# Expert stage of a streaming-encoder trunk: activation turned on VectorE, down products in quarters, combine one item later, gather for four items at once

## The reference

```python
def moe_swiglu(h, w_router, w_gate, w_up, w_down):
    logits = xt @ w_router
    top_logit, top_idx = lax.top_k(logits, TOP_K)          # TOP_K = 2 of 8
    gates = jax.nn.softmax(top_logit, axis=-1)
    ...
    def expert_block(args):
        tok, e = args
        xb = xt[tok]                                       # gather the frames
        return (jax.nn.silu(xb @ w_gate[e]) * (xb @ w_up[e])) @ w_down[e]
    ...
    contrib = y_rows[pos] * gates[:, None]                 # combine
    y = jax.ops.segment_sum(contrib, flat_tok, num_segments=n_tok)
```

## Time and profile before

| | us |
|---|---|
| median of 3 runs | 1605.27 |
| their ends | 1601.61 to 1605.38 |
| the profiled execution | 1601.6 |
| its span, first to last instruction | 1599.8 |

### The profile page before, as it was taken

The page is one execution under the profiler, slowest core; times in us unless marked ns, Lnnn a source line. Parts: engine busy times, 40 slices in busy tenths (PEclk is TensorE's granted clock), DMA queues, the critical chain, the costliest instruction groups (busy, mean ns, idle before and its releaser), DMA issues.

```text
span 1599.8 us, 30459 instructions
## 1 busy us (share of the span) xinstructions
PE 1528.5 (96%) x13157; PEld 844.9 (53%) x13157; DVE 399.6 (25%) x610; ACT 377.0 (24%) x524; POOL 24.0 (1%) x42
## 2 busy tenths in 40 slices
PE   4999899999899869999999999999999999999996
PEld 3977899999799753333333333333333333333332
DVE  3454554444466651001001001001001001001001
ACT  4333544444467521001001001001001001011001
POOL 1000000000011100000000000000000000000000
PEclk9999999999999989999999999999999999999998
DMA  9430555555353357997997998997998998998960
GB/s 301 161 128 19 180 184 185 184 185 184 109 168 106 106 227 291 372 413 298 371 416 296 380 400 300 381 406 299 380 398 306 376 403 298 386 396 300 394 244 28
DMA packets 132553, 438.31 MB, mean 274 GB/s; under 512 B 10602, under 2 KB 63936, under 8 KB 116032
## 3 DMA queue, kind: packets, MB, share of 16 engines
q1 hardware_dynamic: 131232, 432.73, 72.3%
q0 software_dynamic: 1184, 3.50, 0.7%
HBM read 435.15 MB, written 1.05 MB: 273 GB/s over the span
## 4 chain that ended last, share of the span: by engine, by line
PE 93%; DVE 2%; ACT 2%; issue 1%; DMA 1%; SPq 1%; DVEq 0%; POOL 0%; ACTq 0%
PE bank L1121 55%; PE bank L764 9%; PE bank L765 9%; PE bank L766 9%; PE bank L1191 3%; PE bank L1175 2%; PE bank L1154 2%; DMA raw<-in_ev_w_in 1%; PE bank L864 1%; PE bank L757 1%; ACT high L594 1%; DVE hn L1523 0%; SPq L707 0%; DVE low L599 0%; PE bank L1165 0%
## 5 line engine op out<-in xcount | busy, mean ns | idle before, releaser
L1121 PE MATMUL bank<-ring,arena 128*32 128x512 f32 (+1 forms) x8832 | 878.9, 556 | 0.8 <-ACT arena L1404 0.8
L1121 PEld LDWEIGHTS bank<-ring,arena 128*32 128x32 f32 x8832 | 280.4, 110 | 561.3 <-issue 561.3
L599 DVE TENSOR_TENSOR low<-raw,high 128x2048 fp32r<-128x2048 f32 x74 | 169.3, 2290 | 169.5 <-ACT high L594 169.5
L764 PE MATMUL bank<-ht_h,high 128*128 128x256 f32 x672 | 192.5, 287 | 3.0 <-DVE vec L1587 3.0
L765 PE MATMUL bank<-ht_l,high 128*128 128x256 f32 x672 | 191.1, 284 | 0.0
L766 PE MATMUL bank<-ht_h,low 128*128 128x256 f32 x672 | 191.0, 284 | 0.0
L594 ACT ACTIVATE high<-raw 128x2048 fp32r<-128x2048 f32 x74 | 141.5, 1912 | 162.9 <-PE bank L766 158.1
L1898 DVE TENSOR_TENSOR arena<-arena,bank 128x512 f32<-128x512 f32 (+1 forms) x48 | 29.8, 621 | 536.6 <-PE bank L1121 535.1
L764 PEld LDWEIGHTS bank<-ht_h,high 128*128 128x128 f32 x672 | 129.9, 193 | 4.4 <-issue 3.9
L765 PEld LDWEIGHTS bank<-ht_l,high 128*128 128x128 f32 x672 | 130.1, 194 | 0.2
L766 PEld LDWEIGHTS bank<-ht_h,low 128*128 128x128 f32 x672 | 129.9, 193 | 0.0
(11 more groups left out here) (264 smaller groups left out, 1075.1 us busy)
## 6 DMA issues: line engine op xcount, KB each, us to landing
ring<-in_moe_w_down SPq DMA_DIRECT2D x112, 1024.0 KB, 8.0
ring<-in_moe_w_gate SPq DMA_DIRECT2D x64, 1024.0 KB, 7.3
ring<-in_moe_w_up SPq DMA_DIRECT2D x64, 1024.0 KB, 7.0
ring<-in_moe_w_gate SPq DMA_DIRECT2D x64, 768.0 KB, 5.6
ring<-in_moe_w_up SPq DMA_DIRECT2D x64, 768.0 KB, 7.3
raw<-in_ffn_w_gate SPq DMA_DIRECT2D x14, 1024.0 KB, 5.0
raw<-in_ffn_w_up SPq DMA_DIRECT2D x14, 1024.0 KB, 5.0
raw<-in_ffn_w_down SPq DMA_DIRECT2D x14, 1024.0 KB, 4.9
```

The lines of the kernel that those rows point to most:

```text
L599: nc.vector.tensor_tensor(low[:, n % SPLITS, :], raw[:, raw_slot(n), :], high[:, n % SPLITS, :].bitcast(F32), ALU.subtract).then_inc(split ...
L764: mm(out, l_high, r_high, start=start, stop=False)
L1121: ins = mm(ps(use)[q * GRP:(q + 1) * GRP, 0:width], lhs(r, q), rhs(q), start=first, stop=last_piece)
```

## The change

- **Turning.** VectorE transposes the activation in 32x32 blocks straight into `m_act_t` after multiplying it. For that the gate and up products read their weights in runs of 32 columns, quarter by quarter, so that a block holds 32 columns of one quarter. TensorE's `act_transposes` and ScalarE's `turned_acts` go.
- **Down.** Each quarter q now makes 256 output columns over all contraction blocks: 3 groups x 2 blocks x 4 quarters = 24 products of 256 columns for a piece, 48 matmul instructions. One chain of sums over both parts; ScalarE copies three 128x256 results to `y_e`, and `y_first` goes.
- **Combine.** 24 products, 256 wide, with 32 rows of contraction, in the next item behind its second gate piece; the last one stands behind both loops.
- **Gather.** For items 0 to 3 ahead of item 0, for items 4 to 7 inside it, with one-pass products of `hn` split in a high and a low part (384 columns, four for each of eight blocks). VectorE copies an item's rows from `xg_all` to `xg`. The split is a ScalarE copy and a POOL subtraction of 128x2048.
- **Loop.** Item 0 is written out ahead of the loop, `Fori(1, NE)`. Extra items gather on their own (`gather_extra`).

```diff
+DN = DM // NQ
+DOWN_ORDER = (2, 0, 1)
+DOWN_BANKS = {0: 6, 1: 7, 2: 2}
+FIRST_ITEMS = NE // 2
+GATHERED = FIRST_ITEMS * SLOTS
...
@@ TensorE
             def expert_gate_up(j, item):
...
+                weights = ring[:, at:at + NQ * width].rearrange("p (b q i) -> p q b i", q=NQ, i=GRP)
                 pe.wait_ge(*expert_landed(j, item))
-                tiled(product(key), part, key, lambda r, q: xg[:, k, r * GRP:(r + 1) * GRP],
-                      lambda q: ring[:, at + q * width:at + (q + 1) * width], k == 0, width, item)
+                for r in range(NG):
...
+                        ins = mm(ps(use)[q * GRP:(q + 1) * GRP, 0:width], xg[:, k, r * GRP:(r + 1) * GRP],
+                                 weights[:, q, :, :], start=k == 0, stop=k == DK - 1)
...
             def expert_down(j, item):
...
+                for r in DOWN_ORDER:
+                    use = ("md", r)
+                    if j == 4 * DK:
+                        open_bank(pe, use, item)
+                    for c in range(2):
+                        for q in range(NQ):
+                            ins = mm(ps(use)[q * GRP:(q + 1) * GRP, 0:DN], m_act_t[:, r, first + c, :],
+                                     ring[:, at + c * DM + q * DN:at + c * DM + (q + 1) * DN],
+                                     start=j == 4 * DK and c == 0, stop=ends and c == 1)
...
+            def gather(half, k):
+
+                use = ("gather", half, k)
+                open_bank(pe, use)
+                for t in range(T):
+                    for part in (hn_h, hn_l):
+                        last = mm(ps(use)[:, 0:GATHERED], part[:, t, k * P:(k + 1) * P],
+                                  sel_all[:, t, half * GATHERED:(half + 1) * GATHERED],
+                                  start=t == 0 and part is hn_h, stop=t == T - 1 and part is hn_l)
+                last.then_inc(fill_sem(use), 1)
...
+            def combine(item):
+
+                for r in DOWN_ORDER:
+                    pe.wait_ge(*drained(("md", r), item))
                 for half in range(2):
+                    pe.wait_ge(*drained(("sgt", half), item))
                 for t in range(T):
                     for r in range(NG):
+                        for q in range(NQ):
+                            use = ("mc", q)
+                            if t == 0 and r == 0:
                                 open_bank(pe, use, item)
+                            rows = slice(q * GRP, (q + 1) * GRP)
+                            last = mm(ps(use)[:, t * DN:(t + 1) * DN], sgt[rows, r, t * P:(t + 1) * P], y_e[rows, r, :],
+                                      start=r == 0, stop=r == NG - 1)
+                            if t == T - 1 and r == NG - 1:
                                 last.then_inc(fill_sem(use), 1)
...
+                    if first and j < DK:
+                        gather(1, j)
+                    if key == ("g", 0, 1) and not first:
+                        combine(item - 1)
+                    if key == ("u", 0, 0):
+                        pe.wait_ge(sel_ready, item + 1)
+                        turned_selection(0, item)
+                    if key == ("u", 0, 3):
+                        turned_selection(1, item)
...
+            pe.wait_ge(hn_split, 1)
+            pe.wait_ge(all_sel_ready, T)
+            for k in range(DK):
+                gather(0, k)
+            pe.wait_ge(all_sel_ready, 2 * T)
+            pe.wait_ge(xg_ready, 1)
+            expert_item(0, True)
+            with pe.Fori(1, NE) as item:
+                pe.wait_ge(xg_ready, item + 1)
                 expert_item(item)
             pe.wait_ge(route_ready, 1)
             n_items = pe.value_load(route_i[0:1, 0:1], min_val=NE, max_val=NITEM)
             with pe.Fori(NE, NITEM) as item:
                 with pe.If(n_items > item):
+                    gather_extra(item)
                     expert_item(item)
+            combine(n_items - 1)
@@ ScalarE
             norm_banks(3)
+            act.wait_ge(*filled("router_rows"))
+            act.wait_ge(hn_ready, T * 4)
+            fn(hn_h, hn[:, :, :], ACT.Copy).then_inc(hn_high, 1)
             act.wait_ge(r_in, 1)
             fn(r_e, r_e, ACT.Exp).then_inc(r_exp, 1)
@@ POOL
+            pool.wait_ge(hn_high, 1)
+            nc.gpsimd.tensor_tensor(hn_l, hn[:, :, :], hn_h.bitcast(F32), ALU.subtract).then_inc(hn_split, 1)
+            nc.gpsimd.memset(xg_all[:, NE, :], 0.0).then_inc(past_xg_zero, 1)
@@ VectorE
             def gated(part, item):
...
+                for r in range(NG):
+                    dve.wait_ge(*drained(("mu", part, r), item))
+                    V.transpose(m_act_t[:, r, first:first + blocks, :].rearrange("p b c -> p (b c)"),
+                                m_act[:, r, 0:width]).then_inc(turned_ready, 1)
...
+            def next_rows(item, first=False):
...
+                V.tensor_copy(xg.rearrange("p k s -> p (k s)"), xg_all[:, bass.ds(item + 1, 1), :].rearrange(
+                    "p o c -> p (o c)")).then_inc(xg_ready, 1)
...
+            add_contributions(n_items - 1)
             V.memset(r_max, 0.0).then_inc(experts_done, 1)
```

More of the change, by code:

```diff
@@ L211, in ends_a_product @@
     kind, part, k = key
-    return k == (DPAIRS[part] if kind == "d" else DK) - 1
+    if kind == "d":
+        return (part, k) == (len(PARTS) - 1, DPAIRS[part] - 1)
+    return k == DK - 1
 def ring_places():
@@ L317, in plan_banks @@
     banks.fill("rank", 5)
-    for half in range(2):
-        banks.fill(("gather0", half), 6 + half)
+    for k in range(DK):
+        banks.fill(("gather", 0, k), k)
+    for k in range(DK):
+        banks.fill(("gather", 1, k), 6 + k % 2)
     before = list(banks.count), list(banks.signals)
     for half in range(2):
-        banks.fill(("sgt", half), 6 + half)
+        banks.fill(("sgt", half), 7)
     for part in range(len(PARTS)):
@@ L573, in product @@
             kind, part, _ = key
-            return ("m" + kind, part)
+            return ("md", DOWN_ORDER[-1]) if kind == "d" else ("m" + kind, part, NG - 1)
         def expert_landed(j, item):
@@ L1151, in act_transposes, with turned_selection @@
+            def turned_selection(half, item):
+                use = ("sgt", half)
                 open_bank(pe, use, item)
-                pe.wait_ge(*drained(("mu", part, r), item))
-                for j in range(WIDTHS[part] // P):
-                    last = nc.tensor.transpose(ps(use)[:, j * P:(j + 1) * P], m_act[:, r, j * P:(j + 1) * P], ident)
+                for r in ((0, 1), (2,))[half]:
+                    for t in range(T):
+                        at = (r % 2 * T + t) * P
+                        last = nc.tensor.transpose(ps(use)[:, at:at + P], sel_q[:, t, r * P:(r + 1) * P], ident)
@@ L1168, in gather @@
-            def gather(name, item):
-                for half in range(2):
-                    use = (name, half)
-                    open_bank(pe, use, item)
-                    for k in range(4):
-                        for t in range(T):
-                            last = mm(ps(use)[:, k * SLOTS:(k + 1) * SLOTS],
-                                      hn[:, t, (half * 4 + k) * P:(half * 4 + k + 1) * P], sel[:, t, :],
-                                      start=t == 0, stop=t == T - 1)
-                    last.then_inc(fill_sem(use), 1)
@@ L1194, in combine, with expert_item @@
+                            if t == T - 1 and r == NG - 1:
                                 last.then_inc(fill_sem(use), 1)
-            def expert_item(item):
-                for half in range(2):
-                    b, n, _ = uses[("gather", half)]
-                    pe.wait_ge(s_drained[b], n - bank_fills_per_item[b] + item * bank_fills_per_item[b])
+            def expert_item(item, first=False):
                 for j, key in enumerate(EXPERT_ORDER):
                     kind, part, k = key
-                    if key == ("g", 0, 1):
-                        turned_selection(item)
-                    for p, before in ((0, "g"), (1, "d")):
-                        if (kind, part) == (before, 1 - p) and TURN_AT <= k < TURN_AT + NG:
-                            act_transposes(p, k - TURN_AT, item)
@@ L1892, in gated @@
             def gated(part, item):
+                width, first = WIDTHS[part], PARTS[part][0] // P
+                blocks = width // GRP
                 for r in range(NG):
@@ L1905, in expert_item @@
+            def expert_item(item, first=False):
+                if not first:
+                    add_contributions(item - 1)
+                    for half in range(2):
+                        dve.wait_ge(*filled(("sgt", half), item - 1))
+                one_hot(item)
                 gated(0, item)
                 gated(1, item)
-                for r in range(NG):
-                    use = ("md", 1, r)
-                    dve.wait_ge(*drained(("md", 0, r), item))
-                    dve.wait_ge(*filled(use, item))
```

(18 more changed lines are left out.)

216 lines of the change are left out of this document (115 added, 101 removed).

## The result

| | kernel before | changed kernel |
|---|---|---|
| median of 5 runs, us | 1605.27 (1601.61 to 1606.08) | 1612.87 (1610.79 to 1617.59) |
| ratio to before | 1 | 1.0062, interval 1.0048 to 1.0077 |
| profiled execution: time / span, us | 1601.6 / 1599.8 | 1617.59 / 1615.7 |
| mean granted clock | 0.983 | 0.959 |

What follows compares the result with a forecast made beforehand. TensorE, busy 96% of the span, was taken as the bound. Terms -79.4 + 17.4 + 8.5 + 8.0 + 1.7 + 8.5 = -35.3 us gave 1570 us against the median 1605.27, within 1556 to 1584 (0.53).

Steps and rivals of the forecast that it cites:

- The work of a trip: One trip of TensorE's expert loop: the changed parts together take -9.92 us, a trip of 112.5, -79.4 over eight.
- Gathers in item 0: Gathers of items 4 to 7 inside item 0: eight visits of 1.0 us each, +8.0 us.
- The back branch: End of a loop trip on TensorE: branch no longer hidden, gap of 2.9 us, six branches, +17.4 us (ends 0 and 20).
- The half clock: After back-branch gaps: clock at half for 3.4 us costs 1.7, five of six counted, +8.5 us (ends 0 and 20).
- The cover: Work queued behind TensorE's back branch: twenty instructions of 256 columns, five groups, hiding 1.08 us of it.
- Start of the stage: Before item 0: hn split on ScalarE and POOL, then first gathers; item 0 starts +1.7 us later (ends 0 and 4).
- End of the stage: Last combine behind TensorE's walk over the extra items: 7.3 us on the path, 0.5 for waits; sum +8.5 (+5 to +11).
- The branch stays hidden: Rival at the loop's back branch: no gap and no clock drop, 1544 us; chance 0.14.
- DMA as the bound: Rival in the loop: weight transfers take 119.0 us a trip, seven trips add 15, 1585 us; chance 0.10.
- Two at a time: Rival in the combine: its products run no more than two at a time, +20, 1590 us; chance 0.08.
- slow dispatch: Rival in the down pieces: instructions dispatched too slowly for the quarters, 3.87 us a piece, adding 143, 1713 us; chance 0.06.
- slow operand pattern: Rival in gate and up: runs of 32 elements slow the moving operand, 10% gives 1628 us; chance 0.05.

## Why the prediction was wrong

It named the right mechanism, a back branch that loses its cover, and priced it at a third of what it cost (25.9 of 73.2 us). Point by point:

- **The work of a trip: right.** -9.92 gave 112.48 us, measured 112.59. Down pieces 36.26/14 = 2.59 us (forecast 2.593), combine 2.80 (2.79), no transposes but the selection's (0.59 and 0.37), gate and up unchanged at 5.15 for the first two pieces (2 x 2.576). The line from 512 through 384 columns down to 256 held.
- **Gathers in item 0: right.** Item 0 takes 729.13 - 610.99 = 118.1 us; a clean trip without its combine is 112.59 - 2.80 = 109.8; so 8.3 us, forecast 8.0.
- **The back branch: the step that failed.** Forecast 2.9 us of gap and 1.4 of half clock, 4.3 a trip and 25.9 in all. Measured 5.0 + 3.0 + 4.1 = 12.1 in the trip shown, and over the stretch from item 0 to the last down piece 979.88 - 906.73 (branch announced) = 73.2: 30.5 in first gaps, 16.6 in second ones, 26.1 of half clock. Three terms of it were wrong:
  - *The price of the first fetch*, 3.52 us, was taken from rows where the transfers had just stopped (share 0.16). Beside full transfers it is 6.03, because its code packet starts 2.5 us later. With that price the prediction's own formula is right: 6.03 + 0.45 - 1.3 = 5.2, measured 5.02. It had bounded this term by 3.3 above, from the same rows. Miss: 30.5 - 17.4 = 13.1 us.
  - *The second fetch* had no term at all: 16.6 us of gaps, gone with the head at a block's start.
  - *The half clock* was sized from short, thin stretches, 3.4 us at half. Here the clock falls at 845.45, 3.7 us after TensorE's last instruction and still inside the first gap, and is back at 855.7, 10.2 us later; 5 us of work in them took 9.2. Miss: 26.1 - 8.5 = 17.6.

  Together 47.3 of the 51 us.
- **The cover was right**: instructions, not microseconds, and twenty of them. Twenty start after the branch in each of the six trips. They last 1.3 to 1.4 us where 1.08 was forecast, since those already under way have to end first.
- **Start of the stage: wrong**, +5.8 instead of +1.7. "POOL has nothing else queued" looked at POOL's queue and not at VectorE's work beside it. The POOL subtraction took 4.48 us (forecast 5.9), and for that time one VectorE step stood still, 4.56 us instead of 0.23, which put the whole router chain 4.3 us later. The kernel with the subtraction on VectorE gets 3.7 back. The Trainium skill's "SBUF — State Buffer", section "Who interferes with whom", says that a VectorE instruction with two SBUF inputs contends with a GpSimd instruction that reads SBUF, and that the shared ports are an exclusive lock. The trace agrees with that: the two start together and last 4.56 and 4.48 us.
- **End of the stage: right in size.** 7.21 us of wait (forecast 7.3 and 0.5), the combine in 5.11 at the half clock (2.6 more than 2.8 was forecast), the memset at 1606.23, so 1606.23 - 1603.73 = 2.5 us behind it (3.0). From the last down piece on it is +1.4, forecast +2.1.
- **Rivals.** The branch stays hidden: wrong, though its 1544 is what the kernel takes with the branch announced or written out. DMA as the bound: wrong, 391 GB/s were sustained with no gap. Two at a time, slow dispatch, slow operand pattern: wrong, by the pieces above; with 48 matmul instructions in 2.59 us, one is 54 ns. (The 0.16 us from the earlier trace rows, given against slow dispatch, is that of eight weight loads alone; their matmuls are not in that row.) The 62 ns for each MATMUL that the Trainium skill's "TensorE: Matmul & The Clock Gate", section "Wait — 56ns, not 53.3ns?", gives for hardware decode off are not seen here, at 54 ns. That the estimate made from it, 1613 us, is the measured time is chance: the time was lost at the branch, and none of it in the down pieces.
- **The other side.** It gave 0.09 to slower, by dispatch and operand pattern. The mechanism that came true was in the forecast's own sum, with too low an upper end: 20 us for the gaps, where six trips lost 47 to them, and 20 for the clock, which took 26. The Trainium skill's "Runtime: NRT & Kernel Launch", section "Instruction fetch mechanics", says that a taken branch whose target is out of the window has to fetch it by DMA before execution can go on. That it goes through DMA would have been the hint to ask what else the DMA engines do at that moment; the trace agrees, with a code packet in every wait, and 3.4 us beside idle engines and 6.0 beside busy ones.

## What to carry to other kernels

A loop's back branch is hidden only as long as the instructions queued behind it last. Whoever makes the instructions at a trip's end shorter or cheaper has to price the branch anew, and at the DMA load of the place where it will stand, not where it stood; then announce it or write the loop out. Read a price in a trace together with what ran beside it: both large misses, the fetch and the POOL subtraction, were right durations read in the wrong company. The trace has the code packets themselves: the queue of kind "instruction" tells of a branch whether its wait is for code and what the packet stood behind. And when the total hardly moves, compare one clean trip (item 0 to item 1 here, 5.15 us for 48 instructions) with one across the branch (1.92 + 7.31 and two gaps): that alone gives the ledger.

## What was not expected of the hardware

- A taken back branch on TensorE's sequencer costs 3.3 to 3.9 us with nearly idle DMA engines, 6.0 to 6.3 us beside weight transfers at over 400 GB/s, and 0.45 us when it was announced. The parts: 0.9 to 1.5 us until a 16 KB code packet starts (3.5 to 3.8 beside transfers), about 1 us for it, 1.3 to 1.5 us until the branch ends.
- A second code packet follows behind the branch, in the kernel before too. In the changed kernel TensorE waited for it after five matmul instructions, 1.6 to 3.6 us (4.3 to 5.0 where the transfers were held back to meet it). Another place of the loop's head removes the wait.
- With the combine back in its trip, the branch waited for two code packets, 6.6 to 6.9 us.
- A VectorE step of 0.23 us took 4.56 us beside a POOL subtraction of 4.48 us.
- In the branch's first gap, 3.7 us after TensorE's last instruction, the granted clock fell to 0.50 (1.2 GHz) for 10.2 us, and two weight pieces took 9.2 us instead of 5.15.
- Matmul instructions of 256 columns in four column strips go out at 54 ns each, beside as many weight loads, with no loss.
